# Copies of the old value rows move from the prompt attention to the routing's first four dense tiles

## The reference

```python
k_all = jnp.concatenate([state_k_win[l], kb], axis=1)
v_all = jnp.concatenate([state_v_win[l], vb], axis=1)
keep = min(MAX_WINDOW, buf_len + DS)
kws.append(k_all[:, buf_len + DS - keep:])
vws.append(v_all[:, buf_len + DS - keep:])
```

## Time and profile before

| | |
|---|---|
| time, median of 3 runs | 4050.66 us (4045.88 to 4054.15) |
| time of the profiled execution | 4036.62 us |
| its span | 4034.8 us |
| granted PE clock, mean | 0.91 |
| prompt attention, stage | about 399 to 719 us of the span |
| dense tiles of the routing | about 1604 to 2008 us |

### The profile page before, as it was taken

One profiled execution on the slowest core, in us unless ns is written; L12 is line 12 of the kernel. 1 busy time (PEld: TensorE's weight loads), 2 busy tenths in 40 slices (PEclk: granted clock), 3 DMA queues, 4 the chain that ended last, 5 costly groups with the idle time before them and its releaser, 6 DMA issues. The chain is left out here.

```text
span 4034.8 us, 59078 instructions
## 1 busy us (share of the span) xinstructions
PE 3311.0 (82%) x20585; PEld 2890.3 (72%) x20585; DVE 2778.2 (69%) x5881; ACT 1357.6 (34%) x3190; POOL 1709.0 (42%) x1341
## 2 busy tenths in 40 slices
PE   6999688566686892666589999999999999999994
PEld 3677455211376792555489999999999999999993
DVE  3223676100231199999779998999999889999885
ACT  3010466000221111887633333333333333333331
POOL 1010000000212441888765665665565565565560
PEclk7999799777788996776699999999999999999997
DMA  6632546999422331787598998998988988898983
GB/s 232 221 124 74 172 148 212 357 412 406 161 72 77 99 115 42 200 240 205 141 329 318 330 325 303 326 331 311 326 319 314 334 316 314 320 322 307 328 300 148
DMA packets 389552, 1001.89 MB, mean 248 GB/s; under 512 B 187044, under 2 KB 232975, under 8 KB 325688
## 3 DMA queue, kind: packets, MB, share of 16 engines
q1 hardware_dynamic: 323768, 491.18, 35.9%
q0 software_dynamic: 62656, 469.86, 32.2%
q10 hardware_dynamic: 2944, 38.77, 2.6%
HBM read 914.75 MB, written 152.04 MB: 264 GB/s over the span
## 5 line engine op out<-in xcount | busy, mean ns | idle before, releaser
L2174 DVE CUSTOM_DVE_ANT_0 e_uv<-e_uv,e_h 128x1024 f32<-128x1024 f32 x416 | 721.7, 1735 | 73.8 <-DMA e_uv<-peer_uv,k_g_idx 73.1
L2243 POOL DMA_INDIRECT e_uv<-peer_uv,k_g_idx x416 | 521.1, 1253 | 540.4 <-DVE e_pY L2186 496.8
L1475 PE MATMUL e_po<-e_ph,e_vh 128*128 128x320 f32 x2048 | 646.3, 316 | 59.2 <-DVE k_OT L2218 55.1
L1475 PE MATMUL e_pa<-k_hi_d,e_uh 128*128 128x320 f32 x2048 | 638.4, 312 | 50.7 <-POOL e_ul L2234 37.5
L1476 PE MATMUL e_po<-e_pl,e_vh 128*128 128x320 f32 x2048 | 633.3, 309 | 0.0
L1477 PE MATMUL e_po<-e_ph,e_vl 128*128 128x320 f32 x2048 | 633.3, 309 | 0.0
L1477 PE MATMUL e_pa<-k_hi_d,e_ul 128*128 128x320 f32 x2048 | 633.2, 309 | 0.0
L1476 PE MATMUL e_pa<-k_lo_d,e_uh 128*128 128x320 f32 x2048 | 633.1, 309 | 0.0
L2186 DVE SCALAR_TENSOR_TENSOR e_pY<-e_uv,e_wts,e_pY 128x1024 f32<-128x1024 f32 x412 | 526.0, 1277 | 0.0
L1475 PEld LDWEIGHTS e_po<-e_ph,e_vh 128*128 128x128 f32 x2048 | 384.8, 188 | 83.7 <-DVE k_OT L2218 71.3
L1475 PEld LDWEIGHTS e_pa<-k_hi_d,e_uh 128*128 128x128 f32 x2048 | 384.8, 188 | 62.0 <-issue 46.0
(11 more groups left out here) (305 smaller groups left out, 5889.7 us busy)
## 6 DMA issues: line engine op xcount, KB each, us to landing
k_kv<-kv_pages SPq DMA_DIRECT2D x128, 512.0 KB, 7.0
s_kv<-kv_state SPq DMA_DIRECT2D x32, 2048.0 KB
e_v<-peer_uv SPq DMA_DIRECT2D x128, 512.0 KB
e_u<-peer_ut SPq DMA_DIRECT2D x126, 512.0 KB, 6.1
s_g<-r_G SPq DMA_DIRECT2D x10, 4096.0 KB
k_OT<-s_g SPq DMA_DIRECT2D x128, 320.0 KB
v_win_sample<-state_v_win POOLq DMA_DIRECT2D x28, 1168.0 KB, 10.0
k_win_sample<-state_k_win ACTq DMA_DIRECT2D x28, 1168.0 KB
```

Source lines behind the costliest of these rows:

```text
L1475: nc.tensor.matmul(out, lhs_hi, rhs_hi, start=start, stop=False)
L2174: nc.vector.tensor_tensor_reduce(uv[:, r, 0:D], uv[:, r, 0:D], h[:], 1.0, 0.0, ALU.mult, ALU.add, dots[:, r:r + 1]).then_inc(row_dotted, 1)
L2243: nc.gpsimd.indirect_dma_start(uv[:, s % RING], None, io["peer_uv"], bass.IndirectOffsetOnAxis(ap=keep.g_idx[:, s:s + 1], axis=0),).then_i ...
```

## The change

The POOL program of `prompt_attn` goes, with its two semaphores. In `peer_route`, ACT issues a key share after groups 0, 5, ..., 30 as before and now a value share after groups 1, 6, ..., 31, in tiles 0 to 3. The value shares add to the same semaphore, and the wait at the end of `finish` counts 56 shares.

```diff
-        win_out = [nc.alloc_semaphore(f"a_win_out{u}") for u in range(2)]
...
-            @block.gpsimd
-            def _(pool):
-                with pool.Fori(0, WIN_SHARES // 2) as i:
-                    for u in range(2):
-                        copy_window(pool, io, "v", 2 * i + u).then_inc(win_out[u], 16)
-                        pool.wait_ge(win_out[u], 16 * i + 16)
...
-    assert PER_TILE * (ND - 1) == WIN_SHARES and -(-NGT // COPY_EVERY) == PER_TILE
+    assert PER_TILE * (ND - 1) == WIN_SHARES and len(range(1, NGT, COPY_EVERY)) == len(range(0, NGT, COPY_EVERY)) == PER_TILE
...
-                        if i < ND - 1 and g % COPY_EVERY == 0:
-                            copy_window(act, io, "k", PER_TILE * i + g // COPY_EVERY).then_inc(keep.win_out, 16)
+                        if i < ND - 1 and g % COPY_EVERY < 2:
+                            copy_window(act, io, "kv"[g % COPY_EVERY], PER_TILE * i + g // COPY_EVERY).then_inc(keep.win_out, 16)
...
-                sp.wait_ge(keep.win_out, 16 * WIN_SHARES)
+                sp.wait_ge(keep.win_out, 2 * 16 * WIN_SHARES)
```

## The result

| | before | after |
|---|---|---|
| median of 4 runs | 4048.27 us (4045.2 to 4054.15) | 4224.19 us (4214.94 to 4225.85) |
| profiled execution, span | 4034.8 us | 4213.1 us |

What follows compares the result with a forecast made beforehand. In the dense tiles DVE sets the pace, with the eight DMA engines that carry the copies close behind, nothing to spare. Terms -10 + 1 + 130 = +121 us on 4050.66 gave 4172 us; range asked 4060 to 4225.

Steps and rivals of the forecast that it cites:

- 1 and 2: Attention's end and start: without value copies it ends 4.0 us sooner and starts 6 sooner; together -10 us, between -4 and -11.
- 3: Dense tiles: ACT's 28 more issues, 0.69 us each, lie beside activations already started; +1 us, or 19 without that cover.
- 4: Dense tiles: one copy share on the eight engines takes 5.6 us, ends 5.0 and 6.5.
- term 6: Dense tiles: the eight engines' free time, 10 us before the first store, 12 after tile 3, 5 between; 157 - 27 = 130 us.
- (41.4 - 19.4) over some four: Tile 0: a share's time read from a store's 41.4 us wait, less 19.4 alone, over four shares; 5.5 us.
- the other two readings: A share's time on eight engines: 7.2 us from one copy alone, 6.5 us from queue 10's total.
- 5: Tiles 0 to 3: copies beat stores, delaying ACT's `leave`, `make`, then PE and DVE; 28 x 5.6 = 157 us of work.
- 7: Routing: tiles last about 119 us; the load of scores and `finish` cost nothing; tile 4 unchanged.
- Room in the mean: Rival, dense tiles: transfers yield and stores aren't held, so only the attention's gain is left; 4041 us, chance 0.08.
- Sixteen alike: Rival, dense tiles: copies spread over all 16 engines, DMA share 1.10, tiles of 88 us; 4065 to 4073 us, chance 0.12.
- ACT held at the issue: Rival, dense tiles: ACT's queue fills and a copy holds ACT before `make` and `leave`; +230 us, 4280, chance 0.06.

Runs made afterwards that it cites:

- e1: The changed kernel with the value copies left out, key copies kept; 0.9981 of the kernel before (0.9964 to 0.9999), 4024.2 against 4030.35 us.
- e6: The changed kernel with value copies of one row of each share's 73, all issues kept; 0.9984 of the kernel before (0.9967 to 1.0001).
- e9: The changed kernel with each share named as 8 by 292 runs of 128 numbers, packets staying at 37376 bytes; 1.0378 of the kernel before.
- e2: The changed kernel with value copies of 36 of each share's 73 rows, all issues kept; 1.0139 of the kernel before, 4089.9 us.
- e3: The changed kernel with key and value copies cut in quarters of a sequence, spread over sixteen engines; 0.9969 of the kernel before, 4020.1 us.
- e11: The changed kernel with each share as 8 rows of 146 runs of 1024 bytes, same bytes and queue; 1.0441 of the kernel before.
- e5: The changed kernel with the tiles' value copies issued from POOL's queue instead of ACT's, same shares; 1.0329 of the kernel before, +134 us.
- e10: e3 repeated on another chip; 0.9985 of the kernel before (0.9969 to 1.0001), 4029.33 us.

## Why the forecast was right or wrong

1 and 2. **The attention, -10: -13.5.** Timelines of PE and DVE, then SP, in after, against the earlier trace rows:

```profile
408.38 3.77 PE L695 MATMUL a_pT<-k_ident,a_qk 128*128 128x128 f32 x16 [13.66 <-DMA a_qk<-s_proj]
...
705.01 0.29 DVE L800 COPY k_OT<-a_pO 128x128 f32<-128x128 f32 x1 [1.46 <-PE a_pO L738]
706.06 0.33 SPq L922 DMA_DIRECT2D s_O<-s_proj  x1
```

At the start 6.4 us came (7.9 from the first load's issue to the first turn, 14.2 before), 6 forecast. At the end I had counted 4.0; it was 6.6, since the barrier takes 0.8 us from DVE's end, and the 3.3 us that I took for a barrier held most of the last copy's completion. The sum took it for granted that all of this reaches the end of the kernel; e1 shows 6 us, in an interval of 0.4 to 14.5, so that step is neither shown nor refuted.

3. **Issues, +1: none** (e6).

4. **A share at 5.6 us on the eight engines: about 7.5.** This is the term that was mis-sized: the tiles stage grew by 180.9 us where terms 4 to 6 gave 130. By tiles, (132.8 - 79.6) / 7 = 7.6 us; by the stage, (180.9 + 27) / 28 = 7.4 with the free time of term 6. In e9, the same copies on another chip, the stage took 533.2 us, which gives 6.9. Three queue views of after show the parts, at 1728 to 1736, 1738 to 1774 and 1776 to 1784 us:

```profile
q1 hardware_dynamic: 3907, 1.00, 66.0%
q10 hardware_dynamic: 40, 1.20, 49.2%
```

```profile
q10 hardware_dynamic: 214, 6.50, 50.2%
q1 hardware_dynamic: 214, 0.05, 0.7%
```

```profile
q1 hardware_dynamic: 4416, 1.14, 63.1%
```

While the other eight engines are at their half of a store, a share takes 8.0 us (1.20 MB in 8 us); with those idle it takes 6.6 (6.50 MB in 36 us is 181 GB/s). The eight alone finish their half of a store, 2.1 MB, at 142 GB/s, in 14.8 us. A tile is then 4 x 8.0 + 10 x 6.6 + 2 x 14.8 + 3 = 131 us, as measured (131.2 and 134.4). With seven shares it is 4 x 8.0 + 3 x 6.6 + 29.6 + 3 = 84, against 79.6, and with e2's half shares at 3.3 us more 107, against 100. So the sum fits when the eight engines are full and is some 5 to 7 us too high below that.

The error was in "(41.4 - 19.4) over some four": 19.4 us is a store's time with all sixteen engines at it, but eight alone need 14.8, and (41.4 - 14.8) / 4 = 6.7. That rate stood in the earlier trace rows: from 1910 to 1915 us nearly all the packets are the store's, at 142 GB/s. Beside that I took the two fastest of four windows in the earlier trace rows (198 would have given 6.0) and weighed the 6.5 and 7.2 us of the other two readings away as counting overlap or first latency. These too stood in the rows and pointed up.

5. **Copies win over stores, and the chain ACT, PE, DVE: right**, shown by the packet counts and the waits. **6. Free time, 27 us: not settled, rather too small.** With 7.4 us a share, e2's half dose (28 shares of 7.4 x 36/73 = 3.65 us) leaves 28 x 3.65 - 62 = 40 us free; a straight line through the half and the whole dose gives 8.4 us a share and 54 us free. A larger free time and a dearer share offset each other, so the two terms can't be told apart by their sum. **7. Tile 4 unchanged, loads of scores harmless: right** (the last of the seven waits, 25.9 us, is at tile 4's first group, where term 6 had 12 us to spare before; from there to the experts it took 72.4 us, where it was 80.1).

**Rivals.** Room in the mean fell with the sign. Sixteen alike fell with e3: the same bytes on sixteen engines cost nothing. I had priced that rival at 88 us a tile from a share of 1.10; e3 has the share and tiles of 80 us. ACT held at the issue did not happen in the change (its issues took 0.68 us) and did in e11. The share of DMA in these tiles fell, as told: to 0.70 in tiles 1 and 2 from 0.81 and 0.82, where 0.74 was forecast, and to 0.67 from 0.71 over the five tiles.

## What to carry to other kernels

A DMA share is a mean over engines: where it stands at half with a transfer pending, look which access has a slowest size below 16, and spread that before moving it. A copy is not free for having no reader: on its engines it takes turns with everything, packet by packet, so one with large packets starves a transfer of small ones, and in a stage of short loads that are waited for, it holds them even at a share of 0.34. When a shared engine's work is priced by a difference of two times, both must have been taken with the same neighbours running.

## What the runs showed of the hardware that I had not expected

- Eight engines by themselves store at 142 GB/s, but sixteen together at 216 (4.19 MB in 19.4 us), not 284: in stores of 256-byte runs they slow each other.
- The sum of packet times can pass 1 (1.06 to 1.08 in e3) at 328 to 340 GB/s with no stage any slower.
- An issue on ACT takes 0.68 us with copies of four packets an engine unfinished behind it, and up to 9.4 us with copies of 146 (e11).
- POOL's copies over eight engines fall by turns on ACT's eight and on the other eight (e5: ACT's packets take 2.55 us beside the one kind, 1.39 beside the other), while in after never more than eight copy packets were in flight at once, but for 0.2 us in all, however many of ACT's shares were unfinished.
- The Trainium skill, DMA: Bandwidth & Descriptors, "Issuing engines are not separate DMA queues", holds as far as it goes, for which engine issues; but by its section on the count of engines the access decides how many carry it, and that was worth some 180 us here (e3 and e10 at 0.997 and 0.9985 of before, the change at 1.0433).

What stays open: why a share takes 6.6 us with the other engines idle and was as fast as 5.8 in parts of tile 0 (206 GB/s); how the loss divides between the price of a share and the free time; and how much of the attention's 13.5 us reaches the end of the kernel.
